# Both gates of an RG-LRU in one weight array, 64-row products in pairs, and delta rows turned by a transposing DMA, in a Hymba and expert block

## What is computed

```python
h = concat([meta, x])                         # 4112 rows of 1024
xb, gb, q, k, v, z, b_logit, a_logit = split(rmsnorm(h, mix_norm) @ w_in)

xc = causal_conv(xb, conv_w) + conv_b         # 512 channels
xblk = xc.reshape(b, t, 8, 64)
r = sigmoid(einsum('btnc,ncd->btnd', xblk, w_r) + b_r)
i = sigmoid(einsum('btnc,ncd->btnd', xblk, w_i) + b_i)
log_a = -8.0 * r * softplus(-lam)
a, b = exp(log_a), sqrt(-expm1(2.0 * log_a)) * (i * xc)
h_t = a_t * h_(t-1) + b_t
y_lru = rmsnorm(h * gelu(gb), lru_out_norm)

q, k, v = silu(causal_conv(q, k, v));  q, k = l2norm(q), l2norm(k)
# gated delta rule, chunkwise, 4 heads of 128: a unit lower-triangular solve per chunk
y_dn = rmsnorm(o, out_norm) * silu(z)

h = h + concat([y_lru, y_dn]) @ w_out
# top-1 of 4 groups, top-2 of 8 experts in it, a gated MLP (1024 x 256) for each
h = h + moe(rmsnorm(h, ffn_norm))
out = rmsnorm(h, final_norm)[16:]
```

## Time and profile before

| | before |
|---|---|
| runs, us | 3215.45, 3208.48, 3200.05 |
| median, us | 3208.48 |
| the profiled execution, us | 3197.16 |
| its span in the trace, us | 3195.5 |
| mean granted clock of TensorE | 0.969 of full |
| PE busy | 2935.7 us, 92% |
| PEld (weight loads) busy | 2195.9 us, 69% |
| DVE (VectorE) busy | 2554.9 us, 80% |
| ACT (ScalarE) busy | 1973.5 us, 62% |
| POOL (GpSimd) busy | 907.7 us, 28% |
| instructions | 81737 |
| moved by DMA | 396.53 MB |

### The profile page before, as it was taken

One profiled execution on the slowest core, in us unless ns is written; L12 is line 12 of the kernel. 1 busy time (PEld: TensorE's weight loads), 2 busy tenths in 40 slices (PEclk: granted clock), 3 DMA queues, 4 the chain that ended last, 5 costly groups with the idle time before them and its releaser, 6 DMA issues. The chain is left out here.

```text
span 3195.5 us, 81737 instructions
## 1 busy us (share of the span) xinstructions
PE 2935.7 (92%) x28640; PEld 2195.9 (69%) x28641; DVE 2554.9 (80%) x7201; ACT 1973.5 (62%) x4385; POOL 907.7 (28%) x962
## 2 busy tenths in 40 slices
PE   4788999999999999999999999996799999999960
PEld 4777888788878887888788888874344555554530
DVE  6887888888878887888788878876788888888844
ACT  7554666565656566656555565653677777777746
POOL 4422222122212222221222122212344444444420
PEclk9999999999999999999999999998899999999985
DMA  6111232322222222222222222225487877777749
GB/s 231 65 37 32 70 100 72 86 71 75 74 87 68 81 74 81 68 81 76 79 74 74 82 73 80 70 72 211 119 275 223 239 211 199 193 222 217 230 99 394
DMA packets 186113, 396.53 MB, mean 124 GB/s; under 512 B 86992, under 2 KB 86992, under 8 KB 173520
## 3 DMA queue, kind: packets, MB, share of 16 engines
q1 hardware_dynamic: 148896, 286.22, 26.6%
q0 software_dynamic: 29216, 89.30, 12.2%
q10 hardware_dynamic: 7696, 16.86, 1.4%
HBM read 280.05 MB, written 96.01 MB: 118 GB/s over the span
## 5 line engine op out<-in xcount | busy, mean ns | idle before, releaser
L621 PE MATMUL pj<-uT,W 128*128 128x128 f16 x15744 | 974.4, 220 | 12.3 <-POOL W L1939 12.3
L621 PEld LDWEIGHTS pj<-uT,W 128*128 128x128 f16 x15744 | 927.0, 98 | 40.7 <-issue 30.4
L2295 DVE SCALAR_TENSOR_TENSOR W<-W,ecol 128x512 f16<-128x512 f16 x664 | 447.4, 746 | 111.0 <-ACT W L2239 103.1
L2239 ACT ACTIVATE W<-W,ecol 128x512 f16 x664 | 415.8, 708 | 79.2 <-issue 77.0
L2203 PE MATMUL bA<-W,uT 128*128 128x512 f16 x1992 | 447.1, 381 | 5.6 <-issue 4.4
L2203 PEld LDWEIGHTS bA<-W,uT 128*128 128x128 f16 x1992 | 193.6, 98 | 229.1 <-issue 10.0
L2187 PE MATMUL pj<-W,qs 128*128 x664 | 299.8, 594 | 0.9 <-ACT qs L2266 0.9
L2000 POOL TENSOR_TENSOR decb<-upto,nbeta 128x512 f32<-128x512 f16 x33 | 36.1, 1093 | 889.7 <-DVE nbeta L1735 889.7
L1025 ACT ACTIVATE ht<-ht 128x512 f32<-128x512 f32 x256 | 159.2, 623 | 95.2 <-DMA ht<-w_up 89.9
L2187 PEld LDWEIGHTS pj<-W,qs 128*128 128x128 f32 x664 | 119.9, 190 | 120.8 <-issue 120.2
L1055 ACT ACTIVATE qh<-bA 128x256 f32<-128x256 f32 x198 | 76.8, 388 | 191.4 <-PE bA L787 187.7
(11 more groups left out here) (508 smaller groups left out, 6119.8 us busy)
## 6 DMA issues: line engine op xcount, KB each, us to landing
ht<-w_gate SPq DMA_DIRECT2D x128, 256.0 KB, 3.1
ht<-w_up SPq DMA_DIRECT2D x128, 256.0 KB, 3.2
W<-w_gate SPq DMA_DIRECT2D x32, 1024.0 KB
W<-w_up SPq DMA_DIRECT2D x32, 1024.0 KB
W<-w_down SPq DMA_DIRECT2D x32, 1024.0 KB
x_in<-xm SPq DMA_DIRECT2D x33, 512.0 KB, 4.5
ht<-xm SPq DMA_DIRECT2D x32, 512.0 KB, 3.8
h_rows<-ht SPq DMA_DIRECT2D x32, 512.0 KB
```

What stands on the lines that cost most here:

```text
L621: mm = pe.matmul(pj[g % 2][:, j, :], w16[:, k, w_half(w_high, COL[GROUPS[g]], 512, j * P, P)], (ul if low_u else uh)[:, k, :], start=(k == ...
L2239: nc.scalar.activation(part_of(wx[par][:, 0], k), raw[:, k], ACT.Copy, scale=ecol[par][:, k:k + 1]).then_inc(sem("wx_high"), 1)
L2295: a = nc.vector.scalar_tensor_tensor(out=part_of(wx[par][:, 1], k), in0=raw[:, k], scalar=ecol[par][:, k:k + 1], in1=part_of(wx[par][:, 0] ...
```

## The change

**Gates.** One array `w_gates` takes the place of `wr_bd` and `wi_bd`. Its rows 0 to 63 hold the even blocks (channels 0 to 63 of each 128), r in columns 0 to 63 and i in columns 64 to 127; rows 64 to 127 hold the odd blocks, i first and r second. Eight products of 64 rows, alternating between the row halves and between banks bC and bT, stand in one place ahead of the projection run (3,0). Four sigmoids of full width write `even` and four write `odd` (the room decb), with the biases laid out alike in `gcols`. So r lies on the partitions where la wants it, and i on the other half: two DMAs (`gate_rows`) move it into gx. POOL's multiplication by c becomes two on 64 partitions each, one ahead of the product yg and one behind it; the product of gx and xc waits for the DMAs and moves behind the sums of y.

**Delta rows.** `turn_delta` goes. ScalarE writes the high parts and VectorE the low parts row-wise into `yd_rows`, which is the room of ks, and one transposing DMA (`delta_columns`) writes yd16 from it, before the third weight chunk in SP's order. VectorE's convolution of k, which writes ks, waits for it, and so does `w_out_part(4)`.

**ScalarE's order.** The vt copy moves ahead of the norm of h and the xb copy; the squares of chunks 0 and 1 move behind level 5's copy, those of the second expert's chunks 2, 3 and 4 stand together; level 6's copy moves ahead of the tanh.

**Loads of experts.** Step 32 loads the first expert only, and step 33 the other three.

The diff, cut to what matters (the wr_bd and wi_bd loads and memsets go too):

```diff
-        wr_bd = sb("wr_bd", [P, 4, P])
-        wi_bd = sb("wi_bd", [P, 4, P])
+        w_gates = sb("w_gates", [P, 4, P])
+        even = sb("even", [P, 4, P])
...
+        odd = decb
...
+        yd_rows = ks[:].rearrange("p j n -> p (j n)").bitcast(F16)
...
+                for b in range(2):
+                    for n, src in enumerate((w_r, w_i)):
+                        c = 64 * (b ^ n)
+                        sp.dma_start(w_gates[64 * b:64 * b + 64, :, c:c + 64], src.rearrange("(j b) c d -> b c j d", b=2)[b]
+                                     ).then_inc(sem("bd_in"), 16)
+                        sp.dma_start(gcols[c:c + 64, b, :], lru_cols[64 * b:64 * b + 64, 1 + n, :]).then_inc(sem("bd_in"), 16)
...
                             if c == KT - 2 and n == 1:
                                 turned_rows(s)
+                            if c == 2 and n == 0:
+                                delta_columns(s)
+                            if c == 4 and n == 0:
+                                gate_rows(s)
                             if c > 1 or n:
                                 need(sp, sem("w_sq"), s.squares + KT * n + c - 1)
                             src = (w_gate, w_up)[c // 4][bass.ds(s.first + n, 1)].rearrange("o (p k) f -> p (o k f)", k=KT)
                             sp.dma_start(ht[:, 512 * (c % 2):512 * (c % 2) + 512], src[:, 512 * (c % 4):512 * (c % 4) + 512]
                                          ).then_inc(sem(f"w_raw{c % 2}"), 16)
...
+                def delta_columns(s):
+                    if s.O:
+                        need(sp, sem("yd_ready"), s.nO)
+                        sp.dma_start(yd16.rearrange("p s j n -> p (s j) n"), yd_rows, transpose=True).then_inc(sem("yd_full"), 16)
+                def gate_rows(s):
+                    if s.P:
+                        need(sp, sem("gates_out"), 2 * s.nP)
+                        need(sp, sem("h_scan"), s.nG)
+                        sp.dma_start(gx[0:HALF], even[HALF:P]).then_inc(sem("i_moved"), 16)
+                        sp.dma_start(gx[HALF:P], odd[0:HALF]).then_inc(sem("i_moved"), 16)
...
+                    if not s.sums:
+                        delta_columns(s)
+                        gate_rows(s)
...
                         if isinstance(s.i, int) and s.i == TILES - 1:
                             sp.wait_ge(sem("ba_full"), TILES)
-                            for slot in range(WSLOTS):
+                            load_expert(sp, 0, 0)
+                        if isinstance(s.i, int) and s.i == TILES:
+                            for slot in range(1, WSLOTS):
                                 load_expert(sp, slot, slot)
...
-                            need(pe, sem("yd_ready"), s.nO)
+                            need(pe, sem("yd_full"), 16 * s.nO)
...
                     for j in range(4):
-                        mm = pe.matmul(bC[:, j, :], bd[:, j, :], xc[:, j, :], start=True, stop=True)
-                    mm.then_inc(sem(done), 1)
+                        pe.matmul(bC[:, j, :], w_gates[0:HALF, j, :], xc[0:HALF, j, :], start=True, stop=True)
+                        mm = pe.matmul(bT[:, j, :], w_gates[HALF:P, j, :], xc[HALF:P, j, :], start=True, stop=True)
+                    mm.then_inc(sem("gates_full"), 1)
...
-                        mm.then_inc(sem("gr_full"), 1)
+                        need(pe, sem("kd_ready"), s.nG)
+                        gates()
...
-                    if s.P:
-                        need(pe, sem("r_gate"), s.nP)
-                        for j in range(4):
-                            mm = pe.matmul(bC[:, j, :], wi_bd[:, j, :], xc[:, j, :], start=True, stop=True)
-                        mm.then_inc(sem("gi_full"), 1)
...
+                def even_gates(s):
+                    need(act, sem("gates_full"), s.nP)
+                    need(act, sem("i_moved"), 32 * s.pP)
+                    need(act, sem("la_ready"), s.pP)
+                    for j in range(4):
+                        a = nc.scalar.activation(even[:, j, :], bC[:, j, :], ACT.Sigmoid, bias=gcols[:, 0, j:j + 1])
+                    a.then_inc(sem("gates_out"), 1)
+                def odd_gates(s):
+                    need(act, sem("M_raw"), 2 * s.pG + 1 if s.G else 0)
+                    for j in range(4):
+                        a = nc.scalar.activation(odd[:, j, :], bT[:, j, :], ACT.Sigmoid, bias=gcols[:, 1, j:j + 1])
+                    a.then_inc(sem("gates_out"), 1)
...
+                    act.wait_ge(sem("w_split"), len(GROUPS) - 1)
+                    odd_gates(s)
...
+                    if s.G:
+                        need(act, sem("pre_full"), 5 * s.pG + 3)
+                        need(act, sem("vn_full"), s.pG)
+                        nc.scalar.activation(vt[:], bC[:], ACT.Copy).then_inc(sem("vt_ready"), 1)
...
-                        need(act, sem("pre_full"), 5 * s.pG + 3)
-                        need(act, sem("vn_full"), s.pG)
-                        nc.scalar.activation(vt[:], bC[:], ACT.Copy).then_inc(sem("vt_ready"), 1)
...
-                        need(act, sem("yd_full"), s.nO)
-                        nc.scalar.activation(yd16[:, 0], bT[:], ACT.Copy).then_inc(sem("yd_high"), 1)
+                        need(act, sem("yt_ready"), s.nO)
+                        nc.scalar.activation(yd_rows[:, 0:512], flat(yt), ACT.Copy).then_inc(sem("yd_high"), 1)
...
-                    if s.G:
-                        raw_squares(s, 0, twice=(2,))
                     if s.P:
...
-                        raw_squares(s, 1, twice=(3,))
+                        even_gates(s)
+                        odd_gates(s)
                     level_y(s, 5)
                     if s.G:
-                        raw_squares(s, twice=(4,))
+                        raw_squares(s, 0, 1, twice=(2, 3, 4))
                     if s.G:
                         need(act, sem("y_lru"), s.nG)
                         nc.scalar.activation(aa, yg[:], ACT.Square).then_inc(sem("y_sq"), 1)
-                    if s.P:
-                        need(act, sem("gi_full"), s.nP)
-                        need(act, sem("h_scan"), s.nG)
-                        for j in range(4):
-                            a = nc.scalar.activation(gx[:, j, :], bC[:, j, :], ACT.Sigmoid, bias=lcol[:, 2, j:j + 1])
-                        a.then_inc(sem("i_gate"), 1)
                     if s.G:
                         raw_squares(s, twice=(5,))
+                    level_y(s, 6)
...
-                    level_y(s, 6)
...
                     need(dve, sem("yd_high"), s.nO)
-                    nc.vector.tensor_tensor(yd16[:, 1], bT[:], yd16[:, 0], ALU.subtract).then_inc(sem("yd_ready"), 1)
+                    nc.vector.tensor_tensor(yd_rows[:, 512:1024], flat(yt), yd_rows[:, 0:512], ALU.subtract).then_inc(sem("yd_ready"), 1)
...
+                    if s.P:
+                        need(dve, sem("yd_full"), 16 * s.nO)
...
+                def even_decay(s):
+                    need(pool, sem("gates_out"), 2 * s.pP + 1)
+                    need(pool, sem("a_step"), 2 * s.nG)
+                    nc.gpsimd.tensor_tensor(la[0:HALF], even[0:HALF], cl[0:HALF].unsqueeze(2).to_broadcast([HALF, 4, P]), ALU.mult
+                                            ).then_inc(sem("la_even"), 1)
+                def odd_decay(s):
+                    need(pool, sem("gates_out"), 2 * s.nP)
+                    need(pool, sem("la_even"), s.nP)
+                    need(pool, sem("y_lru"), s.nG)
+                    need(pool, sem("scattered"), 32 * s.nS)
+                    nc.gpsimd.tensor_tensor(la[HALF:P], odd[HALF:P], cl[HALF:P].unsqueeze(2).to_broadcast([HALF, 4, P]), ALU.mult
+                                            ).then_inc(sem("la_ready"), 1)
+                    need(pool, sem("la_ready"), s.nP)
+                def gated_input(s):
+                    need(pool, sem("i_moved"), 32 * s.nP)
+                    nc.gpsimd.tensor_tensor(gx[:], gx[:], xc[:], ALU.mult).then_inc(sem("gx_ready"), 1)
...
                         need(pool, sem("M_raw"), 2 * s.pG)
+                        need(pool, sem("i_moved"), 32 * s.pP)
...
+                    if s.P:
+                        even_decay(s)
...
                     if s.P:
-                        need(pool, sem("r_gate"), s.nP)
-                        nc.gpsimd.tensor_tensor(la, la, rows(cl[:]), ALU.mult).then_inc(sem("la_ready"), 1)
...
+                        odd_decay(s)
...
+                    if s.P:
+                        gated_input(s)
```

69 lines of the change are left out of this document (18 added, 51 removed).

## The result

| | before | after |
|---|---|---|
| median, us | 3206.3 (15 runs) | 3214.1 (15 runs) |
| ratio of the two, 95% interval | | 1.0022 (1.0011 to 1.0032) |
| the profiled execution's span, us | 3195.5 | 3215.2 |
| PE, DVE, ACT, POOL busy, us | 2935.7, 2554.9, 1973.5, 907.7 | 2923.1, 2600.0, 1970.6, 939.2 |

One execution among all runs here, of the kernel with the product held, took 6146 us at full clock and stands in no median and no ratio.

The account below looks back on a forecast made before the run. TensorE was taken to bound the mixer step, busy 63.67 of 64 us. Terms: -19.5 (steps) + 3 (steps 0 and 4) + 1.2 (opening) + 14 (drain) = -1.3 us, put at 3207 us on the median; range 3184 to 3228.

Parts of the forecast that it names:

- Thirty steps at -0.65: Mixer steps 1 to 3 and 5 to 31: each 0.65 us shorter, -19.5 us in all.
- The copy of v at 0.37: Regular mixer step: ScalarE's earlier copy of v removes TensorE's wait of 0.37 us at the product with the state.
- The turn on TensorE: Regular mixer step: taking the four delta-row transposes (0.43 us) off TensorE was counted as gaining 0.
- the block's slack (1.2 us): Regular mixer step: the gates block delays TensorE's level 5 product only when longer than about 1.2 us.
- The gate block at 1.1 us: Regular mixer step: the eight paired gate products on TensorE take 1.1 us, bounds 0.9 to 1.8.
- Steps 0 and 4 at +3: Mixer steps squaring two experts: ScalarE waits for the fifth weight chunk ahead of level 6; +0.5 and +2.5 us.
- The opening at +1.2: Kernel's opening: odd sigmoids wait for POOL to empty their room, then a second multiplication; +1.2 us (0 to 3).
- The drain at +14: Mixer's end: the last store of h queues behind nine expert loads, delaying the last second norm; +14 us (+2 to +16).
- the -1.3 of the sum: Whole kernel: all terms together, -1.3 us on the profiled execution's 3197.2.

Follow-up runs that it names:

- the kernel with the product held: The changed kernel with POOL's product of gx and xc also waiting for VectorE's level 6 write; 3210.8 us, 1.0020 against the kernel before.

## Why the prediction was right or wrong

- *Thirty steps at -0.65.* Right for the 26 from step 6 on, -15.9 in all and -0.70 in most, and for step 3 apart from the clock. Step 2 gained nothing (67.61 us against 67.53): its turn waited 2.17 us for VectorE, 1.16 with the product held, and three traces with the product held take 66.6 us there at the same granted clock, 0.95. So it lost a microsecond beside POOL's product, as the steps with the long copy did. Step 1 was 2.6 us slower. It goes with the granted clock: 70.1 to 71.0 us in the six traces where that is 0.90, the kernel before and two with the new gates among them, 72.8 to 73.3 in the three at 0.88, 73.9 to 74.8 in the five at 0.86. All at 0.88 and 0.86 have the new gates; how the change brings the clock down there stays open. The sum had no term for the clock.
- *The parts of the step.* The copy of v at 0.37: 0.33 shown by itself. The turn on TensorE "taken as 0": right by itself, wrong in company. With the gates shortened, its 0.43 us are worth 0.33, as the kernel with the turn on TensorE shows, where TensorE has no wait left ahead of level 5 to take them up. I had the block's slack (1.2 us) right but did not ask what the slack would be with the transposes kept.
- *The gate block at 1.1 us* and its bound of 1.2: both measured. The trace of before held the rate of a pair in the level 7 rows. The drain of TensorE that the Trainium skill names for a change of tiling mode (TensorEngine Tiling, Tiling Modes) is there, at 0.1 us each way, as the level 7 rows had it.
- *Steps 0 and 4 at +3.* The failed step. I wrote that "the fifth chunk can be asked for only after the third is squared", and took the landing, 3.2 us. The third chunk itself is asked for only after SP's wait for the delta rows, 5 us after its room is free: the wait that I had noted ("SP stands in that wait before the third weight chunk") and priced at nothing, because in a regular step ScalarE does not need that chunk soon. Measured: 7.4 us up to the turn of step 5, where 1.8 were forecast: the wait of 5.45 us, some 1.7 of clock behind it and one locked copy, less what the steps gained. 6.5 us come with the old order of squares too.
- *The opening at +1.2:* 1.3, beside 3.6 of clock in this execution.
- *The drain at +14:* 16.5 in this execution; the loads and the store were costed as they ran. But the comparison behind it was incomplete. I took the alternative, loads as before, to be free, and it is not once the transposing DMA delays them by 7 us (63.4 us against 65.7). A reader who had undone the placement on my word would have gained some 2 us at most.
- *The locked copy:* about 5 us in this execution, in no term. I had weighed the rule of the Trainium skill (SBUF — State Buffer, on the shared port pair) on the convolutions, where the rows show 0.6 us lost for each microsecond of POOL, and set it aside. That 0.6 is a mean; taken one by one, the convolution's instructions are drawn out as the copy is. For both the trace agrees with that rule of the Trainium skill: the one that starts first has the pair for its whole instruction. What I missed is that the change moves POOL's product from the middle of the convolution to its end, where the one short copy stands directly ahead of the level 6 write.

Together: to the -1.3 of the sum come 5.6 us for steps 4 and 5, 3.3 for step 1, 2.2 for steps 2 and 3, 2.5 for the drain and 1.0 in the 26 steps (about 4 for locked copies, against 3 that the others gave beyond the forecast), less 0.9 in the last. That is +12 for this pair of executions, leaving out what the opening and the expert stage took beyond the forecast, where the medians say +8. The sum was a draw made of a gain of 20 and a loss of 18, and misses of 2 to 6 us, nearly all on one side, decided the sign. That the time still fell into the range owes more to the width of the range than to the terms.

## What to carry to other kernels

Where a step is bound by a chain over three engines, price parts of a change in company: two parts that are each worth nothing may be worth a third of a microsecond together, and one of them alone may only cost. A wait put into the DMA queue is paid by whatever stands behind it in the step that needs that queue most, here the steps with two experts and the last two, not the regular one. And where a transposing DMA pays in thirty steps and costs in two, use it in the thirty.
